# Output norms of two mixers moved out of the stage behind the third, on one core

## The reference

```python
y = (y_f + y_b + d_skip[:, None] * xs).reshape(b, t, D_SSD) * silu(z)
y_ssd = _group_norm(y, norm_g, SSD_GROUPS, center=False)            # 2 groups of 256
...
y_rwkv = _group_norm((o_f + o_b), norm_g, RWKV_HEADS, center=True) * gate   # 4 heads of 64
...
y_ml = _group_norm((h_f + h_b), norm_g, MLSTM_HEADS, center=True) * sigmoid(o)   # 4 heads of 64
...
y = concatenate([y_ssd, y_rwkv, y_ml]) @ w_out
x = x + g1 * y
```

## Time and profile before

| | us |
|---|---|
| median of 3 runs | 2301.24 |
| lowest and highest of them | 2297.8, 2306.55 |
| the profiled execution | 2307.51 |
| its span, first to last instruction | 2305.8 |
| PE busy | 2129.9 (92% of the span) |
| DVE, ACT, POOL busy | 836.0, 774.3, 735.9 |
| mean granted clock of PE | 0.962 of full speed |

### The profile page before, as it was taken

One profiled execution on the slowest core, in us unless ns is written; L12 is line 12 of the kernel. 1 busy time (PEld: TensorE's weight loads), 2 busy tenths in 40 slices (PEclk: granted clock), 3 DMA queues, 4 the chain that ended last, 5 costly groups with the idle time before them and its releaser, 6 DMA issues.

```text
span 2305.8 us, 46139 instructions
## 1 busy us (share of the span) xinstructions
PE 2129.9 (92%) x20590; PEld 1974.0 (86%) x20590; DVE 836.0 (36%) x1385; ACT 774.3 (34%) x1368; POOL 735.9 (32%) x539
## 2 busy tenths in 40 slices
PE   4999999888789999999979989988888899999999
PEld 4999766778589999999979987667867899999998
DVE  4755265554641111011148443555455311110112
ACT  3535553323333222121144364433332422222212
POOL 4333161324123333333313322522242233333331
PEclk7999998999899999999989999899998899999999
DMA  7454201000012222234335431010001122222222
GB/s 250 147 156 128 63 8 37 6 2 3 19 55 65 80 76 74 74 110 142 104 87 174 148 114 30 1 38 5 3 2 46 50 79 74 74 74 74 73 76 71
DMA packets 260497, 166.67 MB, mean 72 GB/s; under 512 B 29938, under 2 KB 234228, under 8 KB 260300
## 3 DMA queue, kind: packets, MB, share of 16 engines
q1 hardware_dynamic: 259846, 163.59, 23.9%
q10 hardware_dynamic: 454, 0.14, 0.0%
HBM read 159.59 MB, written 4.12 MB: 71 GB/s over the span
## 4 chain that ended last, share of the span: by engine, by line
PE 84%; DVE 7%; ACT 5%; issue 2%; POOL 1%; DMA 0%; another core or an unknown queue 0%; SPq 0%; DVEq 0%; ACTq 0%
PE PS L928 21%; PE PS L929 20%; PE PS L930 20%; PE PS L1317 5%; PE PS L892 2%; PE PS L1462 1%; PE PS L1146 1%; PE PS L1383 1%; PE PS L1335 1%; PE PS L1183 1%; PE PS L989 1%; DVE U L2330 1%; PE PS L1197 1%; POOL ring_r L810 1%; PE PS L1150 1%
## 5 line engine op out<-in xcount | busy, mean ns | idle before, releaser
L928 PE MATMUL PS<-rwp_r,whi_r 128*128 128x320 f32 x2880 | 904.5, 314 | 40.4 <-POOL ring_r L810 16.5
L930 PE MATMUL PS<-rwp_r,ring_r 128*128 128x320 f32 x2880 | 896.6, 311 | 0.0
L810 POOL TENSOR_TENSOR ring_r<-ring,whi_r 128x1024 fp32r<-128x1024 f32 (+1 forms) x204 | 498.5, 2445 | 1139.7 <-ACT whi_r L1647 1139.7
L929 PE MATMUL PS<-arena_r,whi_r 128*128 128x320 f32 x2240 | 697.4, 311 | 0.0
L928 PEld LDWEIGHTS PS<-rwp_r,whi_r 128*128 128x128 f32 x2880 | 547.0, 190 | 56.0 <-issue 28.6
L930 PEld LDWEIGHTS PS<-rwp_r,ring_r 128*128 128x128 f32 x2880 | 546.9, 190 | 0.0
L929 PEld LDWEIGHTS PS<-arena_r,whi_r 128*128 128x128 f32 x2240 | 425.4, 190 | 0.0
L1647 ACT ACTIVATE whi_r<-ring 128x1024 fp32r<-128x1024 f32 (+1 forms) x204 | 211.4, 1039 | 542.1 <-PE PS L930 542.0
L929 PE MATMUL PS<-U_r,whi_r 128*128 128x320 f32 x960 | 298.2, 311 | 0.0
L2542 DVE TENSOR_TENSOR U<-arena,PS 128x640 f32<-128x640 f32 x44 | 36.2, 822 | 549.7 <-PE PS L930 549.7
L929 PEld LDWEIGHTS PS<-U_r,whi_r 128*128 128x128 f32 x960 | 181.8, 189 | 0.0
(11 more groups left out here) (383 smaller groups left out, 2667.7 us busy)
## 6 DMA issues: line engine op xcount, KB each, us to landing
ring<-in_ffn_w SPq DMA_DIRECT2D x120, 512.0 KB, 3.8
rwp<-in_ada_w SPq DMA_DIRECT2D x64, 512.0 KB, 4.8
ring<-in_w_in SPq DMA_DIRECT2D x50, 512.0 KB, 4.4
U<-in_ada_w SPq DMA_DIRECT2D x16, 512.0 KB, 9.7
ring<-in_w_out SPq DMA_DIRECT2D x16, 512.0 KB, 4.6
arena<-in_ada_w SPq DMA_DIRECT2D x16, 512.0 KB, 4.7
ring<-in_ffn_w SPq DMA_DIRECT2D x16, 384.0 KB, 3.3
out<-arena SPq DMA_DIRECT2D x5, 512.0 KB, 2.6
```

The source lines that it names most:

```text
L810: g.tensor_tensor(rings_r[:, slot_of[n], 0:size(n), :], slot(n)[:, 0:size(n), :], whis[:, q_ % 2, 0:size(n), :].bitcast(F32), ALU.subtract ...
L928: mm(out, w[0][:, k, :], hi[:, cols], start=start, stop=False)
L929: mm(out, w[0][:, k, :], lo[:, cols], start=False, stop=False)
L930: return mm(out, w[1][:, k, :], hi[:, cols], start=False, stop=stop)
```

## The change

The norms of SSD and mLSTM no longer wait for RWKV's end.

- mLSTM: `normalise(c)` adds the two directions in token-major form, takes off the head's mean, and sums squares by head on DVE (five more operations of 128 x 256), into columns of `YN` (token x 30: 10 for SSD, 20 for mLSTM). `mlstm_back` is then two transposes where it was four matmuls.
- SSD: POOL's gate product is done by chunk in the chunk loop (`gate`), ACT squares it (`y_squares`), and PE sums the squares in RWKV's step 0: 20 matmuls with a 128x128 stationary tile and one column of ones.
- At the end of step 0 ACT takes the roots, in step 1 DVE the reciprocals of 128 x 30, in step 2 PE turns them to 30 x 128 and DVE copies them out (`YNT`). SP stores them to DRAM (`yn_d`) and loads them back, broadcast over the partitions: two rows for SSD (`RBS`, in `whi`), two of mLSTM over each half of the partitions (`ring_rows`, in the buffers of w_out's block 2 and the start of 3). SP's loads of these two blocks queue behind it and wait for y_done 6, in step 4.
- DVE scales the row tiles between its additions: SSD's tiles 0 and 1 and mLSTM's two in steps 2 and 3 behind `adds(3, 5)`, SSD's tile 2 at the end of step 2, tile 3 in step 3. In step 4 DVE does mLSTM's gate and the first two `y_low` where the other steps have `prep_scan`, and three more `y_low` behind later additions. ACT does three `y_high` at the end of step 3 and three in step 4.
- Behind RWKV only its own bonus, mean, squares, root, reciprocal of 128 x 320 and scaling are left, and PE does them between row tiles of w_out's blocks 0 and 1, whose order is now SSD's four, mLSTM's two, RWKV's two.

```diff
                     def gates():
-                        pool.wait_ge(s["yt_read"], at["yt_read"] + NC)
-                        pool.wait_ge(s["ys_read"], at["ys_read"] + NC)
-                        g.tensor_tensor(U[:, XS:XS + 4, :], U[:, XS:XS + 4, :], U[:, Z:Z + 4, :], ALU.mult).then_inc(
-                            s["gated"], 1)
-                        pool.wait_ge(s["gated"], at["gated"] + 1)
-                        pool.wait_ge(s["rw_ready"], at["rw_ready"] + 1)
+                        pool.wait_ge(s["yn_mm"], at["yn_mm"] + 1)
...
+                    def gate(c):
+                        pool.wait_ge(s["ys_read"], at["ys_read"] + c + 1)
+                        g.tensor_tensor(U[:, XS:XS + 4, ck(c)], U[:, XS:XS + 4, ck(c)], U[:, Z:Z + 4, ck(c)],
+                                        ALU.mult).then_inc(s["gated"], 1)
...
                         for c in range(2, NC):
                             scaled_values(c)
                             skip(c)
+                            gate(c - 2)
+                        for c in range(NC - 2, NC):
+                            gate(c)
...
                         for f in range(2):
-                            for d in range(2):
-                                ins = mm(PS[:, 6, f * P:(f + 1) * P], YM[:, d, f * P:(f + 1) * P], ident[:, :],
-                                         start=d == 0, stop=d == 1)
+                            ins = tr(PS[:, 6, f * P:(f + 1) * P], YM[:, 0, f * P:(f + 1) * P], ident[:, :])
...
+                        if k == 0:
+                            pe.wait_ge(s["rw_tok"], at["rw_tok"] + 2)
+                            pe.wait_ge(s["ysq_ready"], at["ysq_ready"] + NC)
+                            for c in range(NC):
+                                for q in range(4):
+                                    n = NC * (q // 2) + c
+                                    ins = mm(PS[:, 0, n:n + 1], U[:, Z + q, ck(c)], ones[:, 0:1], start=q % 2 == 0,
+                                             stop=q % 2 == 1)
+                            ins.then_inc(s["yn_mm"], 1)
+                        if k == 2:
+                            pe.wait_ge(s["rw_tok"], at["rw_tok"] + 2 * 2 * k + 2)
+                            pe.wait_ge(s["yn_rec"], at["yn_rec"] + 1)
+                            tr(PS[0:6 * NC, 0, 0:P], YN[:, :], ident[:, :]).then_inc(s["yn_mm"], 1)
...
+                    def norm_rows():
+                        sp.wait_ge(s["yn_read"], at["yn_read"] + 2)
+                        load(yn_d[lay].rearrange("r (c t) -> (r c) t", c=NC), YNT, s["yn_in"])
+                        sp.wait_ge(s["yn_in"], at["yn_in"] + 16)
+                        load(RBS, yn_d[lay][0:2].unsqueeze(0).broadcast_to((P, 2, T)), s["yn_in"])
+                        for q in range(2):
+                            load(ring_rows(lay)[64 * q:64 * q + 64],
+                                 yn_d[lay][2 + q:6:2].unsqueeze(0).broadcast_to((64, 2, T)), s["yn_in"])
+                        sp.wait_ge(s["y_done"], at["y_done"] + 6)
...
+                            if i == 4 and c > 1:
+                                y_squares(c - 2)
...
+                        v.tensor_tensor(YS, YM[:, 0], YM[:, 1], ALU.add).then_inc(s["dve_step"], 1)
+                        dve.wait_ge(s["dve_step"], step())
+                        v.tensor_reduce(YMEAN, heads(YS, 4), AX.X, ALU.add).then_inc(s["dve_step"], 1)
+                        dve.wait_ge(s["dve_step"], step())
+                        v.scalar_tensor_tensor(out=heads(YM[:, 0], 4), in0=wide(YMEAN, 64), scalar=-1.0 / 64,
+                                               in1=heads(YS, 4), op0=ALU.mult, op1=ALU.add).then_inc(s["ym_ready"], 1)
+                        dve.wait_ge(s["ym_ready"], at["ym_ready"] + c + 1)
+                        v.tensor_tensor(YM[:, 1], YM[:, 0], YM[:, 0], ALU.mult).then_inc(s["dve_step"], 1)
+                        dve.wait_ge(s["dve_step"], step())
+                        v.tensor_reduce(YN[:, 2 * NC + c::NC], heads(YM[:, 1], 4), AX.X, ALU.add).then_inc(
+                            s["dve_step"], 1)
...
                         adds(0, 1)
                         if k < NC - 1:
                             prep_scan(k + 1)
+                        else:
+                            for f in range(2):
+                                v.tensor_tensor(U[:, MV + f, :], U[:, MV + f, :], U[:, MO + f, :],
+                                                ALU.mult).then_inc(s["y_done"], 1)
+                            for n in range(2):
+                                y_low(n)
...
                             adds(3 + l, 5 + 2 * l)
+                            if l == 0 and k == 2:
+                                dve.wait_ge(s["yn_in"], at["yn_in"] + 16 * 4)
+                                ssd_scaled(range(2))
+                            if l == 0 and k == 3:
+                                for f in range(2):
+                                    ins = y_scale(MV + f, "mlstm_norm_g", f, ring_rows(lay)[:, f])
...
+                    for f in range(2):
+                        g_job(2 * f, [(BO[:, :], U[:, Z + f, :])]).then_inc(s["g_mm"], 1)
                     w01 = [split_block(Q_WOUT + m) for m in range(2)]
+                    out_rows(range(3))
+                    pe.wait_ge(s["g_src"], at["g_src"] + 1)
+                    for f in range(2):
+                        g_job(2 * f, [(BO[:, :], U[:, BT_ + f, :])]).then_inc(s["g_mm"], 1)
+                    out_rows(range(3, 4))
...
+                    out_rows(range(4, 6))
...
+                    out_rows(range(6, 8))
```

More of the change, by code:

```diff
@@ L504, in _ @@
                             sp.wait_ge(s["yt_read"], at["yt_read"] + NC)
+                        if blk == (lay, "w_out", 2):
+                            norm_rows()
                         if blk == (lay, "w_out", RING):
@@ new lines, in _ @@
+                    ins.then_inc(s["g_mm"], 1)
+                    out_rows(range(4, 6))
+                    pe.wait_ge(s["g_rec"], at["g_rec"] + 1)
+                    for f in range(2):
+                        for hf in range(2):
+                            rows = slice(64 * hf + 32 * f, 64 * hf + 32 * f + 32)
+                            ins = mm(PS[:, 2 * f + hf, 0:HALF], SPREAD[rows, :], gtmp[rows, 3, 0:HALF], start=True,
+                                     stop=True)
+                        ins.then_inc(s["g_mm"], 1)
@@ L1819, in _, with y_high @@
                             ins.then_inc(s["bc_exp"], 1)
+                    def y_high(seq):
+                        act.wait_ge(s["rw_feat"], at["rw_feat"] + 2 * NC)
+                        act.wait_ge(s["rs_dve"], at["rs_dve"] + 2 * NC)
+                        for n in seq:
+                            act.wait_ge(s["y_done"], at["y_done"] + n + 1)
+                            A(rp_r[:, YSEQ[n], :], U[:, YTILES[YSEQ[n]], :], ACT.Copy).then_inc(s["y_hi"], 1)
                     def decays(k):
@@ L1835, in _ @@
                     decays(0)
+                    for c in range(NC - 2, NC):
+                        y_squares(c)
                     for k in range(NC):
@@ L1901, in _ @@
+                    act.wait_ge(s["g_mm"], at["g_mm"] + 5)
+                    A(gtmp[:, 3, 0:HALF], PS[:, 0, 0:HALF], ACT.Sqrt, bias=eps[:, 2:3], scale=1.0 / 64).then_inc(
+                        s["g_std"], 1)
+                    y_high(range(6, 8))
                     for k in range(KT):
@@ L2461, in _ @@
                             chunk_start(k + 1)
+                        if k == 2:
+                            ssd_scaled([2])
+                    y_low(5)
                     def pair(ap):
@@ L2515, in _ @@
-                    y_low(7)
+                        centre(BT_ + n, 2 * n, 3 + n)
+                    dve.wait_ge(s["g_std"], at["g_std"] + 1)
+                    v.reciprocal(gtmp[:, 3, 0:HALF], gtmp[:, 3, 0:HALF]).then_inc(s["g_rec"], 1)
+                    for f, gate in enumerate((LORA, MISC)):
+                        y_ = U[:, BT_ + f, :]
+                        dve.wait_ge(s["g_mm"], at["g_mm"] + 6 + f)
+                        v.scalar_tensor_tensor(out=pair(y_), in0=pair(y_), scalar=col(lay, "rwkv_norm_g", f),
+                                               in1=PS[:, 2 * f:2 * f + 2, 0:HALF], op0=ALU.mult,
+                                               op1=ALU.mult).then_inc(s["dve_step"], 1)
+                        dve.wait_ge(s["dve_step"], step())
+                        v.tensor_tensor(y_, y_, U[:, gate, :], ALU.mult).then_inc(s["y_done"], 1)
@@ L2517, in residual @@
+                    for n in range(6, 8):
+                        y_low(n)
                     def residual(b, m, row, sem):
```

169 lines of the change are left out of this document (83 added, 86 removed).

## The result

The changed kernel takes **2331.7 us** (median of four runs, 2318.9 to 2335.9) against 2299.6 us for the kernel before beside it (2297.8 to 2306.6): ratio **1.0135, 95% interval 1.0102 to 1.0169**. It is slower by 31 us; forecast were 2293 us and no measurable change. The profiled execution took 2328.95 us.

A forecast was written before the change was run, and what follows sets the result against it. PE bounds the kernel (84% of the chain), so DVE or POOL work costs only where PE runs dry. Terms sum to -4.6 us per layer, -4.0 with an allowance, twice -8.0: 2293 us from 2301.24, range 2281 to 2305.

The forecast's parts named there:

- rival (C): Chunk loop: PE waits longer for DVE, a second half-clock stretch per layer costs 6 us: 2305 us, chance 0.16.
- Stage behind RWKV: From the bonus matmuls to w_out's last of 96: ends at 610.1 instead of 628.6, gain 18.5 us per layer.
- The five operations: DVE's additions to normalise(c): 0.45 us each, ym_ready 1.35 us later, three chunk borders at +1.5 us.
- The shorter turning: Two transposes for four matmuls in mlstm_back: gains 1.3 us at the border of chunks 2 and 3 only.
- ACT's squares: Chunk loop: delay the last products of chunk 4 by 0.6 us; earlier ones hide behind e_rows.
- Step 0: RWKV's first step: norm_sum's 20 one-column matmuls take 4.1 us on PE, making the step 2.4 us later.
- Step 4: RWKV's last step: two gates and two y_low on DVE beside POOL's bonus chain, 4.8 us late, bounds 1.0 and 5.8.
- the rule of turns: Step 4: a DVE instruction with two SBUF inputs waits out POOL's, so their streams alternate; 4.8 us late instead of 1.0.
- rival (A): No price for DVE beside POOL, whether DVE keeps the port or the pieces miss each other: 2281 us, chance 0.27.
- The norm rows' way: Through DRAM in step 2: rows land between 486.7 and 506, needed at 495.5; taken as hidden, at the fast end.
- rival (B): Norm rows land late in step 2, at the small load's rate, and DVE stops: +10.5 us per layer, 2314 us, chance 0.07.
- Rest of the span: Time outside the chunk loops, RWKV's steps and the stages behind RWKV: forecast difference 0.

The follow-up runs named there:

- e4: The kernel before with only the five DVE operations added in normalise(c), on a scratch tile: 2318.6 us, ratio 1.0065.
- e13: The kernel before with the five DVE operations on a scratch tile and two transposes of the first direction instead of four turning matmuls: 2338.3 us, ratio 1.0182.
- e7: The changed kernel with the turning in mlstm_back done as four f32 matmuls again, each of two written twice: 2308.1 us, ratio 1.0047.
- e10: The kernel before with mlstm_back turning only the first direction, by two transposes instead of four matmuls: 2297.9 us, ratio 0.9994.
- e2: The changed kernel with ACT's squares of chunks 0 to 2 left out, the five DVE operations kept: 2330.1 us, ratio 1.0110.
- e6: e5 with ACT's squares also issued ahead of its wait for the rows of i = 4: 2294.2 us, ratio 0.9996.
- e8: e6 with the 20 one-column matmuls of step 0 issued earlier, in place of eight matmuls that kept TensorE busy: 2281.2 us, ratio 0.9941.
- e9: e8 with POOL's bonus chain moved from step 4 to behind the keys of step 3: 2274.1 us, ratio 0.9893.
- e5: The changed kernel with the five DVE operations moved behind the next chunk's first four weights, the turning moved with them: 2302.7 us, ratio 0.9992.
- e14: The changed kernel with two matmuls that add zeros in w_rows(c, 3), just ahead of each border: 2311.7 us, ratio 1.0058.

## Why the prediction was wrong

The step that failed is the clock of the chunk loop: the sum holds it at nothing, and rival (C), which names the mechanism (PE waiting longer for DVE, a second stretch at half clock), allows one more stretch per layer, 6 us, with a chance of 0.16. By the mean clocks of the loops the time at the half level went from 2 x 0.11 x 87.6 = 19 us to 2 x 0.31 x 108.1 = 67 us in the first, and from 17 to 55 in the second. The loops grew by 39.7 us where 12.8 were forecast. The sum of all terms without the clock was -8 and the estimate above says -10, but that estimate is good to several us and some of the terms were off both ways, so the agreement is partly luck. Point by point:

- **Stage behind RWKV**: forecast 30 us, measured 30.6 and 28.5. Right, with the two waits that it named.
- **The five operations**: forecast 0.45 each, measured 0.42, up to 0.83 beside POOL. With four matmuls at the border they cost 9.1 and 6.8 us a layer (e4); the terms of the sum for that case, four borders at 1.5 and the 0.9 and 1.0, make 7.9. Right.
- **The shorter turning**: booked as a gain of 1.3 at one border. This is the term that was misread. With the five operations beside it, it takes the clock down (e13 against e4, e7 against the changed kernel); taken alone it changes the kernel's time by nothing that can be told (e10).
- **ACT's squares**: 0.6 and else nothing. No effect found (e2, e6).
- **Step 0**: forecast +2.4; the step grew by 4.2 and 5.7. Forty records took 5.81 us, not 4.1: at the full level they start 0.11 us apart, which would be 4.5, and the clock halved within them. So the price was nearly right and the clock, again, was missing. Moving them away gave all of it back to step 0 (e8).
- **Step 4**: forecast +4.8, by turns. From that step's diagonal products to the bonus matmuls it is +1.9 and +3.3, and four operations took 4.3 us, not 6.5. DVE waited for POOL once (the first gate, 1.52 us), the other three took 0.81, 1.33 and 0.81 beside a POOL operation that went from 1.88 to 2.98. So the rule of turns, by which every operation waits, failed here and held in e9's step 3. The row that it came from was misread, too: POOL was not idle beside L2393 but began 0.04 us after it, so the undisturbed operation was the one that came first. Over-sized; rival (A) had half of it.
- **The norm rows' way**: rows ready at 500.97, the loads issued from 502.36 on and landed by some 510, first needed at 517.45; DVE did not wait. Right: rival (B) did not come. The page of the Trainium skill that the prediction cites here gives its figures for transfers that GpSimd issues; these are SP's, and they landed 1.3 us (the store), 5.0 and 6.3 us (the loads) behind their issue.
- **Rest of the span**: forecast 0, measured +5.3 in the profiled execution. The clock can account for it: by the granted clocks of the traces, the time at the half level outside of loops, steps and stages went from about 84 to 100 us. No run separates it.

The norm rows, timeline of the changed kernel:

```profile
500.70 0.27 DVE L2487 COPY whi<-PS 30x128 f32<-30x128 f32 x1
501.00 0.34 SPq L430 DMA_DIRECT2D yn<-whi  x1
...
502.36 0.34 SPq L430 DMA_DIRECT2D whi<-yn  x1
...
517.45 1.68 DVE L2452 SCALAR_TENSOR_TENSOR U<-U,PC,whi 128x640 f32<-128x640 f32 x2
```

and the issues there, with KB each and us to landing:

```profile
whi<-yn SPq DMA_DIRECT2D x1, 640.0 KB, 5.0
ring<-yn SPq DMA_DIRECT2D x2, 320.0 KB, 6.3
yn<-whi SPq DMA_DIRECT2D x1, 15.0 KB, 1.3
```

**Open**: why the later falls come after stretches in which PE was busy for 6.55 of 6.8 us, in e9 even for all of 6.9. So waits at the border are not needed for every fall; whether the first one starts a swing that then goes on by itself is not shown. The runs show which edits move the clock, not the rule by which it falls. Also open is how much of the pair's effect is the longer wait and how much the missing work. POOL's gates in the loop were not tried apart; e13 shows the fall without them, though a smaller one in the profiled execution (loops of 205.4 us together, against 214.8).

## What to carry to other kernels

Where TensorE waits for another engine in a loop, its clock is a term of the sum: look for the half level in the loop before, and give a change there a case in which most of the loop goes to half clock (67 of 108 us here), not only its own microseconds. Work taken from TensorE in front of such a wait can cost more than it saves; put the added work of the other engine where that engine idles (e5), and only if that cannot be done fill the wait (e14). Small matmuls are priced by their records at either level of the clock, and belong where TensorE waits anyway (e8).

## What the runs showed of the hardware

- Two edits that leave the clock alone one by one (0.964 and 0.964, beside 0.964 and 0.966 of the kernel before) take it to 0.953 together, beside 0.968: 28 (14 to 42) us more than their product.
- More work on TensorE made the kernel faster: four turning matmuls in place of two transposes, 23 us (20 by the ratios); two matmuls that add zeros, 20 us (18). The Trainium skill, "TensorE: Matmul & The Clock Gate", section "A second HAM failure mode: psum-queue depth-cycling", describes short idle times between groups of matmuls that make the clock swing. The rows at 332 to 376 are a swing with 0.25 us of idle in 6.8 us ahead of a fall; e9's second loop is one with no idle time ahead of the fall, which that account does not cover.
- The same program has two paces: loops of 85.5 and 101.0 us in one execution of e9, with the same instructions.
- A one-column f32 matmul with 128x128 stationary is two records, 0.11 us apart at the full level and 0.21 at the half level: 0.22 and 0.43 us.
- A DVE stream with two SBUF inputs and a POOL stream hold each other up, and it is not always the same one that waits. In the changed kernel's step 4 POOL's two scalings went from 3.75 to 5.06 us and DVE's four operations from 3.1 to 4.3; in e9's step 3 two DVE scalings took 6.61 us in place of 1.8 beside two POOL products that took 2.89 and 3.36.
